# Applying the pre-norm's row factor behind the projections instead of in the transposes, in a fused fp32 four-block kernel

## What is computed

```python
# first model, one layer (D=1024, 8 heads of 64, conv branch, D_FF=2816)
h = rms_norm(x, norm1_g);  q, k, v, u = split(h @ w_in)
x = x + concat([moba_attention(rope(q), rope(k), v), conformer_conv(u)]) @ w_out
h = rms_norm(x, norm2_g)                                   # stage f1
x = x + (silu(h @ w_gate) * (h @ w_up)) @ w_down
# second model, layer 0: forgetting attention
h = rmsnorm(x, mix_pre_gain[0])                            # stage fp
q, k, v, gate, f = split(h @ fox_w_in)
m = attention_with_decay(rms(q), rms(k), v, cumsum(log_sigmoid(f + b_f))) * sigmoid(gate)
x = x + rmsnorm(m @ fox_w_out, mix_post_gain[0])           # pm0
h = rmsnorm(x, ffn_pre_gain[0])                            # stage f2
x = x + rmsnorm(swiglu(h), ffn_post_gain[0])               # pf0
# layer 1: S5 state-space mixer
u = rmsnorm(x, mix_pre_gain[1]) @ s5_w_in                  # stage s
y = gelu(ssm(u) + d_skip * u);  m = (y * sigmoid(y @ w_glu)) @ w_out
x = x + rmsnorm(m, mix_post_gain[1])                       # pm1
h = rmsnorm(x, ffn_pre_gain[1])                            # stage f3
x = x + rmsnorm(swiglu(h), ffn_post_gain[1])               # pf1
```

## Time and profile before

| | |
|---|---|
| runs, us | 1065.54, 1067.79, 1068.34 (median 1067.79) |
| profiled execution, us | 1066.74, span 1064.90 |
| mean granted TensorE clock | 0.981 of full |
| PE / PEld / DVE busy, us | 1019.4 / 896.8 / 607.6 |
| ACT / POOL busy, us | 476.4 / 344.0 |
| DMA | 186.9 MB, mean 175 GB/s |
| chain that ended last | PE 74%, DVE 12%, POOL 4%, issue 4%, ACT 4%, DMA 1% |

### The profile page before, as it was taken

The page is one execution under the profiler, slowest core; times in us unless marked ns, Lnnn a source line. Parts: engine busy times, 40 slices in busy tenths (PEclk is TensorE's granted clock), DMA queues, the critical chain, the costliest instruction groups (busy, mean ns, idle before and its releaser), DMA issues.

```text
span 1064.9 us, 16913 instructions
## 1 busy us (share of the span) xinstructions
PE 1019.4 (96%) x6942; PEld 896.8 (84%) x6942; DVE 607.6 (57%) x604; ACT 476.4 (45%) x621; POOL 344.0 (32%) x325
## 2 busy tenths in 40 slices
PE   7999799999999998999999999999989999999997
PEld 5986679999988776877779999987867979999985
DVE  3899665555555444454566755445576555555444
ACT  4762345444443355455454434433434453434432
POOL 4790056888889504130039910000100010000000
PEclk9998799999999999999999999999999999999999
DMA  9641025666677746454445655555980435555540
GB/s 356 206 153 55 1 80 178 212 207 207 209 225 242 235 143 198 119 158 129 148 140 163 193 159 196 190 186 191 377 326 16 160 127 190 187 175 190 192 163 40
DMA packets 130034, 186.86 MB, mean 175 GB/s; under 512 B 4672, under 2 KB 103488, under 8 KB 129344
## 3 DMA queue, kind: packets, MB, share of 16 engines
q1 hardware_dynamic: 105696, 158.34, 45.6%
q10 hardware_dynamic: 24288, 27.81, 7.9%
HBM read 174.60 MB, written 15.73 MB: 179 GB/s over the span
## 4 chain that ended last, share of the span: by engine, by line
PE 74%; DVE 12%; POOL 4%; issue 4%; ACT 4%; DMA 1%; POOLq 0%; SPq 0%; ACTq 0%; DVEq 0%
PE ps L365 11%; PE ps L367 11%; PE ps L366 11%; PE ps L408 7%; PE ps L410 7%; PE ps L412 7%; DVE cacc L1668 4%; PE ps L382 4%; PE ps L384 3%; PE ps L383 3%; DVE wlo L351 3%; PE ps L438 2%; POOL otmp L639 2%; ACT whi L345 2%; POOL ob L653 2%
## 5 line engine op out<-in xcount | busy, mean ns | idle before, releaser
L351 DVE TENSOR_TENSOR wlo<-wraw,whi 128x2048 fp32r<-128x2048 f32 x145 | 349.9, 2413 | 321.6 <-ACT whi L345 321.4
L345 ACT ACTIVATE whi<-wraw 128x2048 fp32r<-128x2048 f32 x145 | 277.6, 1914 | 285.2 <-PE ps L412 140.6
L365 PE MATMUL ps<-actH,whi 128*128 128x256 f32 x1232 | 350.5, 284 | 1.1 <-DVE wlo L351 1.1
L366 PE MATMUL ps<-actL,whi 128*128 128x256 f32 x1232 | 348.7, 283 | 0.0
L367 PE MATMUL ps<-actH,wlo 128*128 128x256 f32 x1232 | 348.7, 283 | 0.0
L365 PEld LDWEIGHTS ps<-actH,whi 128*128 128x128 f32 x1232 | 236.4, 192 | 3.7 <-issue 2.0
L366 PEld LDWEIGHTS ps<-actL,whi 128*128 128x128 f32 x1232 | 236.5, 192 | 0.0
L367 PEld LDWEIGHTS ps<-actH,wlo 128*128 128x128 f32 x1232 | 236.5, 192 | 0.0
L497 POOL TENSOR_SCALAR rs<-ss 128x1 f32<-128x1 f32 (+2 forms) x26 | 8.9, 341 | 655.4 <-ACT nat L480 535.2
L408 PE MATMUL ps<-whi,gH 128*128 128x512 f32 x264 | 82.0, 392 | 0.0
L410 PE MATMUL ps<-wlo,gH 128*128 128x512 f32 x264 | 81.4, 389 | 0.0
(11 more groups left out here) (320 smaller groups left out, 1389.4 us busy)
## 6 DMA issues: line engine op xcount, KB each, us to landing
wraw<-in_ffn_w_gate SPq DMA_DIRECT2D x22, 1024.0 KB, 5.3
wraw<-in_ffn_w_up SPq DMA_DIRECT2D x22, 1024.0 KB, 5.3
wraw<-in_ffn_w_down SPq DMA_DIRECT2D x22, 1024.0 KB, 4.9
wraw<-in_fox_w_in SPq DMA_DIRECT2D x16, 1024.0 KB, 5.4
wraw<-in_w_gate SPq DMA_DIRECT2D x11, 1024.0 KB, 5.3
wraw<-in_w_up SPq DMA_DIRECT2D x11, 1024.0 KB, 5.7
wraw<-in_w_down SPq DMA_DIRECT2D x11, 1024.0 KB, 4.9
wraw<-in_w_in SPq DMA_DIRECT2D x10, 1024.0 KB, 7.2
```

The source lines that it names most:

```text
L345: act.activation(self.whi[:, n0 % RING, :], self.wraw[:, n0 % RAW, :], ACT.Copy).then_inc(self.hi_done, 1)
L351: dve.tensor_tensor(self.wlo[:, n0 % RING, :], self.wraw[:, n0 % RAW, :], self.whi[:, n0 % RING, :].bitcast(F32), ALU.subtract).then_inc(s ...
L365: pe.matmul(out, wh, self.actH[:, k, :], start=(i == 0), stop=False)
L366: pe.matmul(out, wh, self.actL[:, k, :], start=False, stop=False)
```

## The change

For f1, fp, f2, s and f3 the row factor is no longer in the transposes. `n1` keeps the old way.

- **Turn.** `pe_turn_plain` transposes x as it is, waiting for quarters of x (row tile by column half), with filler of 128 columns (`warm`: 8 and 16 matmuls, in f1 and fp 0 and 10). Row tile 1 of the last two column tiles is transposed inside the first unit, at its third and fourth step (`late`). `residual` and the update in `dve_postnorm` run in halves of 512 columns, each with its count.
- **Factor.** ACT squares x behind the turn (`act_pre_squares`), POOL writes the factor to a new `rx`. In f1, f2, f3 DVE makes `rdiag` behind the second unit's split, PE spreads it over all partitions with one matmul of ones against it (`pe_spread`, in the middle of the first up unit), ACT copies that back (`act_spread`), and in each pair DVE multiplies the gate bank by it into `sg` (`gscaled`) before ACT's silu, which then works in place. The up half stays unscaled: the factor of a row goes through the down projection, so fp's residual and pf0's and pf1's post-norm multiply by `rx` instead. In s the spread goes behind the second unit and DVE copies all four banks of u with it. In fp, `block_out` and the forget logits use `rx`.
- **Order.** ACT converts the second unit's weights ahead of the turn. The pair's ACT list is conversion, silu, conversion; DVE's is scaling, split, product, split. POOL's table block 0 stands ahead of f1's norm. In fp the split of the second unit and of the forget weights stands between the sixth and the seventh tile of the turn, and banks are changed (turn in 4, 5, 6, 7, 2, 3; first block in 0, 1). The filler ahead of each of the five turns is gone.

```diff
+    def pe_turn_plain(self, pe, st, ready, banks, warm=(4, 8)):
+        spare = self.tp_spot(KT - 1, banks)[:, (RT - 1) * P:RT * P]
+        def fill(count):
+            for _ in range(2 * count):
+                pe.matmul(spare, self.identb[:], self.identb[:], start=True, stop=True)
+        def one(kt, r):
+            last = pe.transpose(self.tp_spot(kt, banks)[:, r * P:(r + 1) * P],
+                                self.x[:, r, kt * P:(kt + 1) * P], self.ident[:])
+            if r == RT - 1:
+                last.then_inc(self.sem(st + "_transposed"), 1)
+        def late(kt):
+            pe.wait_ge(*self.past(st + "_act_ready", kt - 5))
+            one(kt, 1)
+        fill(warm[0])
+        for c, kts in ((1, (0, 1, 2, 3)), (2, (6, 7))):
+            pe.wait_ge(*self.past(ready, c))
+            for kt in kts:
+                one(kt, 0)
+        fill(warm[1])
+        pe.wait_ge(*self.past(ready, 3))
+        for kt in range(4):
+            one(kt, 1)
+        pe.wait_ge(*self.past(ready, 4))
+        for r in range(RT):
+            for kt in (4, 5):
+                one(kt, r)
+        return {2: lambda: late(6), 3: lambda: late(7)}
+    def pe_spread(self, pe, st, bank):
+        pe.wait_ge(*self.past(st + "_diag", RT))
+        pe.matmul(self.ps[:, bank, 0:TOK], self.ones[:], self.rdiag[:]..., start=True, stop=True)
+    def act_spread(self, act, st, bank):
+        act.wait_ge(*self.past(st + "_spread", 1))
+        act.activation(self.rdiag[:]..., self.ps[:, bank, 0:TOK], ACT.Copy)
...
     def act_pair(self, act, st, n0, a, f0, it=0, f_step=0):
-        act.wait_ge(self.used, n0 + 4 * it + 1)
-        if f0 > 0:
-            act.wait_ge(*self.past(st + "_prod", f))
-        act.activation(self.sg[:], self.ps[:, a, :], ACT.Silu)
         self.split_high(act, n0 + 2, it)
+        if f0 == 0:
+            self.act_spread(act, st, 0)
+        act.wait_ge(*self.past(st + "_gscaled", f + 1))
+        act.activation(self.sg[:], self.sg[:], ACT.Silu)
         self.split_high(act, n0 + 3, it)
...
     def dve_pair(self, dve, st, n0, a, f0, it=0, f_step=0):
-        self.split_low(dve, n0 + 2, it)
+        dve.wait_ge(self.used, n0 + 4 * it + 1)
+        if f0 > 0:
+            dve.wait_ge(*self.past(st + "_prod", f))
+        else:
+            self.split_low(dve, n0 + 2)
+            dve.wait_ge(*self.past(st + "_spread_out", 1))
+        dve.tensor_tensor(self.sg[:]..., self.ps[:, a, :]..., self.rdiag[:]...to_broadcast([P, 2, TOK]), ALU.mult)
+        if f0 > 0:
+            self.split_low(dve, n0 + 2, it)
...
# POOL
-            m.pool_rstd(pool, "f1", D, "f1_squares")
...
             m.pool_prep(pool, 0)
+            m.pool_rstd(pool, "f1", D, "f1_squares", out=m.rx)
...
# ACT, stage fp
-            for r in range(RT):
-                m.act_squares(act, "fp", m.x[:, r, :], r, *m.past("fp_x_ready", r + 1))
             for i in range(2):
                 act.wait_ge(*m.past(f"prep_stored{i}", 48 * (NBLK // 2) + 1))
             act.dma_start(m.wf[:], ...)          # and three more
-            m.act_turn(act, "fp", (0, 1, 2, 3, 4, 5), gain=MIXPRE)
             m.split_high(act, first["fox"] + 1)
+            m.act_turn(act, "fp", (4, 5, 6, 7, 2, 3), gain=MIXPRE, between={6: forget_high})
+            m.act_pre_squares(act, "fp", "fp_x_ready")
...
# ACT, stage f2 (s and f3 alike)
-            m.act_norms(act, "pm0", "f2", 4, "o2_first", n + 4)
+            m.act_post_squares(act, "pm0", 4, "o2_first", n + 4)
+            m.split_high(act, n + 5)
             m.act_turn(act, "f2", (0, 1, 2, 3, 6, 7), gain=FFNPRE)
-            m.split_high(act, n + 5)
+            m.act_pre_squares(act, "f2", "pm0_x_ready")
             m.act_ffn(act, "f2", 4)
...
# PE, stage f2 (s and f3 alike)
-            m.keep_warm(pe, 3)
-            m.pe_turn(pe, "f2", (0, 1, 2, 3, 6, 7))
-            m.pe_ffn(pe, "f2", 4)
+            late = m.pe_turn_plain(pe, "f2", "pm0_x_ready", (0, 1, 2, 3, 6, 7))
+            m.pe_ffn(pe, "f2", 4, late)
...
# DVE, stage f2 (s and f3 alike)
             m.dve_postnorm(dve, "pm0", 4, m.gb[0], "gain0_in", 16)
-            m.dve_scale(dve, "f2")
             m.dve_turn(dve, "f2", (0, 1, 2, 3, 6, 7), gain=FFNPRE)
             m.split_low(dve, n + 5)
+            m.dve_scale(dve, "f2")
             m.dve_ffn(dve, "f2", 4)
```

More of the change, by code:

```diff
@@ L360, in mm_features @@
             for i, k in enumerate(order):
+                if late and f == 0 and i in late:
+                    late[i]()
                 if ready is not None and f == 0:
@@ L367, in mm_features @@
                 last = pe.matmul(out, wl, self.actH[:, k, :], start=False, stop=(i == KT - 1))
+            if f == 0 and middle:
+                middle()
         last.then_inc(self.used, 1)
@@ L386, in mm_quarter, with mm_half_k @@
             last.then_inc(self.used, 1)
-    def mm_half_k(self, pe, n0, banks, half, ready=None):
+    def mm_half_k(self, pe, n0, banks, half, ready=None, late=None):
         for k in range(4):
+            if late and k in late:
+                late[k]()
             self.mm_quarter(pe, n0, banks, half, k, ready)
@@ L454, in pe_turn, with act_turn @@
             last.then_inc(self.sem(st + "_transposed"), 1)
-    def act_turn(self, act, st, banks, n=KT, gain=None):
+    def pe_turn_plain(self, pe, st, ready, banks, warm=(4, 8)):
[27 more added lines that the diff above has]
+        pe.wait_ge(*self.past(st + "_diag", RT))
+        pe.matmul(self.ps[:, bank, 0:TOK], self.ones[:], self.rdiag[:].rearrange("p r t -> p (r t)"),
+                  start=True, stop=True).then_inc(self.sem(st + "_spread"), 1)
+    def act_spread(self, act, st, bank):
+        act.wait_ge(*self.past(st + "_spread", 1))
+        act.activation(self.rdiag[:].rearrange("p r t -> p (r t)"), self.ps[:, bank, 0:TOK], ACT.Copy)\
+           .then_inc(self.sem(st + "_spread_out"), 1)
+    def act_turn(self, act, st, banks, n=KT, gain=None, between=None):
         for kt in range(n):
+            if between and kt in between:
+                between[kt]()
             act.wait_ge(*self.past(st + "_transposed", kt + 1))
@@ L462, in act_turn, with dve_turn @@
                .then_inc(self.sem(st + "_high_ready"), 1)
-    def dve_turn(self, dve, st, banks, n=KT, gain=None):
+    def dve_turn(self, dve, st, banks, n=KT, gain=None, between=None):
         for kt in range(n):
+            if between and kt in between:
+                between[kt]()
             dve.wait_ge(*self.past(st + "_high_ready", kt + 1))
@@ L481, in act_squares, with act_post_squares, act_pre_squares @@
            .then_inc(self.sem(st + "_squares"), 1)
[L483 removed]
+    def act_post_squares(self, act, st, base, first, used):
         for r in range(RT):
[L486 to L490 removed]
+            act.wait_ge(*(self.past(first, 1) if r == 0 else (self.used, used)))
+            act.activation(self.nat[:, r, :].rearrange("p (a b) -> p a b", a=2), self.acc_row(base, r), ACT.Square,
+                           scale=self.rx[:, r:r + 1] if st[:2] == "pf" else 1.0,
+                           accum_out=self.ss[:, r:r + 1]).then_inc(self.sem(st + "_squares"), 1)
+    def act_pre_squares(self, act, st, ready):
+        for r in range(RT):
+            self.act_squares(act, st, self.x[:, r, :], r, *self.past(ready, 2 * r + 2))
     def pool_rstd(self, pool, st, mean_of, ready, cols=None, out=None):
@@ L1794, in _ @@
             dve.wait_ge(*m.past("fb_in", 16))
-            c(dve.tensor_tensor(m.fl[:, 0], ps[:, 0, 0:2 * H2].rearrange("p (r h) -> p r h", r=2),
-                                m.fb[:].unsqueeze(1).to_broadcast([P, RT, H2]), ALU.add))
+            dve.wait_ge(*m.past("fp_rstd", RT))
+            for r in range(RT):
+                c.step(dve.scalar_tensor_tensor(m.fl[:, 0, r, :], ps[:, 2, H2 * r:H2 * r + H2], m.rx[:, r:r + 1],
+                                                m.fb[:], ALU.mult, ALU.add))
+            c.wait()
             dve.scalar_tensor_tensor(m.fl[:, 1], m.fl[:, 0], -1.0, m.fl[:, 0], ALU.mult, ALU.max)\
```

183 lines of the change are left out of this document (98 added, 85 removed), and 4 rows, old and new, of the table KINDS.

## The result

The changed kernel takes 1058.38 us (median of 5 runs, 1055.96 to 1060.29) against 1067.79: a ratio of 0.9914, 95% interval 0.9901 to 0.9927. It is faster, by 9.2 to 9.4 us, where 13.9 were forecast. The median lies at the very end of the range of 1048.0 to 1058.5; by the ratio the time is 1067.79 x 0.9914 = 1058.6 us, just outside it. The profiled execution took 1057.54 us, span 1055.40, clock 0.983.

The account below looks back on a forecast made before the run. TensorE, busy 1019.4 of 1064.9 us, was taken as the bound, with only waits and filler at five turns to win: 2.7 + 2.3 + 3.2 + 2.7 + 3.2 - 0.25 = 13.9 us, forecast 1053.0, range 1048.0 to 1058.5.

Parts of the forecast that it names:

- f1: Turn after the first model's output projection: first unit 3.5 us earlier, less 0.44 spread and 0.4 GpSimd contention; gain 2.7 us.
- fp: Turn ahead of the attention's projections: ScalarE's store wait, DMA issues and conversion come first; first matmul at 376.4, gain 2.3 us.
- f2: Feed-forward turn after the attention: the norm chain leaves TensorE's path, gain 3.65 us less the spread, so 3.2 us.
- s: Turn between f2 and f3: same as f2, less 0.5 us for ScalarE waiting on glu weights; gain 2.7 us.
- f3: Last of the five turns: the same as f2, gain 3.2 us.
- the 0.44 us spread: One added TensorE matmul spreading the row factor, priced from the same shape at L1184, not waiting: cost 0.44 us.
- GpSimd against VectorE: Ahead of f1: the moved table block slows VectorE's weight splits, between 0 and 0.9 us; 0.4 taken.
- rival 1: Clock falls in the new holes: only fp, 1.7 us, 1054.6; all five turns, 1061.3; chance 0.15.
- The store's landing: Ahead of fp's turn: last table store, issued at 368.59, lands 2.8 us later, at 371.4.
- Rival 3: Turn still late: another ScalarE wait, on a weight unit or post-norm squares, leaves half the gain; 1060, chance 0.07.
- End: Last post-norm: a split update and a three-operand multiply add 0.25 us.
- Rivals 2 and 4: 2: more gained in fp, s, f1, 1048.6, chance 0.1. 4: scaling slows every pair, 1072.8 at 0.6 us, chance 0.03.

Follow-up runs that it names:

- e7: Changed kernel with GpSimd's two memsets and first table block put back behind the row factor of f1: 1060.83 us, ratio 0.9940.
- changed family: The changed kernel with all its edited forms, twelve profiles in all; medians from 1053.97 to 1064.32 us.
- first repeat: The changed kernel run and profiled again, unchanged: 1058.34 us, ratio 0.9899.
- e3: Changed kernel with ScalarE's conversion of the second unit's weights in fp moved between the turn's sixth and seventh tile: 1053.97 us, ratio 0.9864.
- both reorderings: Changed kernel with fp's conversion behind six tiles of the turn and s's second glu conversion behind the four copies of turned inputs: 1054.40 us, ratio 0.9866.

## Why the prediction was wrong, and where it was right

- **f2, f3, f1: right.** 3.04, 3.24 and 2.61 us against 3.2, 3.2 and 2.7. The pace of the low parts, the cut update, the 0.44 us spread and the order of ScalarE's conversion all held; f2's hole was named as about 5 us and is 5.12.
- **s: the mechanism right, the 2.60 us against 2.7 partly luck.** With s unedited and its filler in place, seven profiles gain 1.35 to 2.75 us, 2.1 on average; the 0.5 us taken for ScalarE's wait ahead of its copies was 0 in three and 0.4 to 1.1 in four. It follows the landing of the second glu unit, which ScalarE converts ahead of its copies: landed by 30.1 us after f2's last down matmul, no wait; at 30.4, 30.5, 30.7 and 31.1 us, waits of 0.38, 0.48, 0.70 and 1.11. The longest (with fp's DMAs late):

```profile
770.42 0.44 PE L1369 MATMUL ps<-ident,Ur 128*128 128x128 f32 x2 [1.11 <-ACT Ur L1668]
```

And a copy of u with the factor takes VectorE 1.07 to 1.16 us, not the 0.69 us of a plain copy that the sum took, so the seam to the chunk transposes is longer (TensorE's wait there is 1.16 us, was 0.88).
- **GpSimd against VectorE: right, and mis-argued in part.** 0.4 was taken for the overlap; o1's last matmul came 0.53 us later relative to its first. What the text did not see is that the block had to move: without it 5.6 us of wait (e7).
- **fp: the step that failed.** The forecast took the hole left in fp (2.7 us of idle TensorE) to cost nothing but itself, at full clock; the clock fell behind it and the whole stage gained nothing. The first matmul came at 376.44 where 376.4 was forecast, but that agreement is luck: the changed kernel reached the turn 0.38 us earlier, and the hole shrank by 1.92 us, not 2.3. The fall was rival 1, "only fp", priced at 1.7 and given 0.15; it happened in six of the seven profiles of the changed family that keep ScalarE's order in fp, in none of the five with it reordered (idle 0.35 to 1.25 us), and costs 1.5 to 1.7 us (e7 against the others). The argument against it was one wait of 2.08 us without a fall. A hole of 2.58 us, ahead of 419.28, was in the same trace, and the clock fell behind it (from 420.5 to 423.9 us here), as it did in all six profiles of before:

```profile
419.28 1.11 PE L785 MATMUL ps<-ident,ka 128*66 128x128 f32 x8 [2.58 <-ACT kt L797]
420.60:423.90 3.30, 3.22 (x16) 2.36 (x16) 0.47 (x1) 2.01 (x4) 0.00 (x0) 0.50 0.48 116
```

A mean clock by slices hides it. Of the 2.4 us that fp fell short some 1.6 is the fall, 0.4 the store (it landed after 3.1 us where 2.8 was taken, and the hole is 5.49 where 5.07 was worked out), and 0.4 lies behind the first matmul even at full clock: 0.3 is the first tiles running at VectorE's pace (5.8 us to the forget matmuls where 5.56 was), 0.1 is spread over the rest.
- **The store's landing was taken as a constant.** 2.8 us were one execution's. From the store's issue to the wf load behind it, four of the seven profiles with ScalarE's order kept have 2.9 to 3.2 us and three (the filler in fp, no filler, more spreads) 5.5 to 6.2, and then fp is 2.9 to 4.3 us longer than before the change. The three in which the conversion alone was moved still have the store ahead of the turn, and show 2.9 to 3.1. In all six profiles of the kernel before it landed within 2.7 to 3.1 us; why it is late at times in the changed kernel is not shown, and six profiles don't rule it out before. There the norm's chain hid the wait (the load went out 4.3 us after the store); the change put it on the path, with four DMA issues and a conversion behind it. This is the wait that took the place of the one removed. Rival 3, another wait of ScalarE with half the gain lost, was the nearest to it, at 0.07; its examples did not include the store.
- **The start: not a step of the sum, but 2.2 us of the 4.3 by which the table falls short.** It was measured against the earliest of six starts. The medians of the times hold less of it: o1 began at 149.3 on average in six profiles of before, and at 149.7 in twelve of the changed family. The late stores and s's waits can fill its place there; how the five runs of the result divide between them is not known, as one of them was profiled.
- **End: mis-sized.** 0.25 us lost was forecast, nothing was measured.
- **The attention: not in the sum, and 0.5 us longer at equal clock**, as the first repeat shows; the first profile hid it by lacking the fall.
- **Rivals 2 and 4 fell.** No loss in every pair: VectorE's low parts with GpSimd in the way cost TensorE 1.3 us in all of f2, and 1.1 before; TensorE's waits for L743 are 1.8 us in all against 2.1.

With e3's one moved line the forecast 1053.0 is nearly met: 1053.97 there, 1054.40 with both reorderings. All five kernels with fp reordered have medians of 1053.97 to 1055.84, below both kernels.

## What to carry to other kernels

When a long chain across engines is removed, list everything that the waiting engine's queue holds ahead of the step that is now first, and move behind it whatever isn't needed yet: a store's landing, DMA issues, a conversion. Filler ahead of a wait of unknown length can end too early, as it did in fp; shortening the wait was what worked. Treat a DMA's landing as a range over executions. And profile the kernel before more than once before pricing a few microseconds: here its start alone moved by 4.

## What the runs showed that I had not expected

- A TensorE wait of 2.2 to 3.2 us may or may not be followed by a half-clock stretch, in the same kernel at the same place. The hole of 2.20 us in s was followed by one in 13 of 18 profiles; the hole of 2.58 or 2.76 us ahead of the attention's third pair in all six of before but in six of eleven of the changed family without filler there. The Trainium skill, TensorE: Matmul & The Clock Gate, Part 1, says that the window over which the clock gate watches TensorE is free-running, so that the point where the clock changes depends on where in it the work begins. That one place goes either way fits this, and the rows tell no more.
- The price of a fall depends on what runs in it: 1.5 to 1.7 us under dense matmuls, 0.8 to 1.2 at the attention.
- Where no clock event or late store falls in, a stretch repeats almost exactly: f1's 220.8 us within 0.06 us in eight profiles. Much of the spread between profiles is a few discrete events: a hole at the start, a fall, a late landing.
